# Order of one gate's last weight steps, and the slots of four small pieces, in the mLSTM heads of a hybrid layer

## The chip, the cores and the metric

One core of one Trainium2 chip runs one launch. The metric is the device time of that launch in microseconds. TensorE (PE in the profile) multiplies, VectorE (DVE) and ScalarE (ACT) prepare its operands and take its results, GpSimd (POOL) does a little, and the sync engine (SP) issues the loads of the weights.

## What is computed

One decoder layer on 256 tokens of width 4096: an RMSNorm, one wide input projection, two groups of heads (four mLSTM heads and a sparse attention), each with a SiLU gate, an output projection, the residual and a final RMSNorm. The change touches only the mLSTM heads. What one of these needs, cut from the reference:

```python
proj = rmsnorm(x, norm_gain) @ w_in
(m_q, m_k, m_v, m_o, m_z, m_i, m_f, ...) = split(proj)
qk = silu(causal_conv(concat(m_q, m_k), w_conv))        # four taps
# per head: 256 columns of q and of k, 512 of v, of the output gate m_o and of the other gate m_z
s   = (q @ k.T) * exp(dlog - m)                          # scores with the decay
num = s @ v ;  qn = sum(s)
h   = num / max(|qn|, exp(-m))
h   = sigmoid(m_o) * h
h   = h * rsqrt(mean(h * h) + eps) * mlstm_norm_gain
y_m = h * silu(m_z)
x   = x + concat(y_m, y_a) @ w_out
```

## The kernel before

Every large product is in float32 made of three passes: a matrix is kept as a high part and a low part (`hi` and `lo`), and TensorE adds high by high, high by low and low by high. The weights come as one long row of steps, each 128 by 1024 numbers (512 KB, two tiles of 512 columns), through a ring of four places (`RING`). SP loads a step into `w_raw` once DVE has done with the step four before it, ACT writes its high part into `w_hi` once TensorE has used the step four before it (`split`, L1253), and DVE writes the low part (`lo`, L1775). TensorE then uses it for both tiles of 128 tokens: an "eight", 4 products of 3 passes, 12 matmuls. In the loops ACT and DVE are three steps ahead of TensorE (`LOOKAHEAD`): at slot r they treat the weights of step r + 3, and then the small pieces that are written at slot r. TensorE issues the pieces that are written at step r ahead of step r's own matmuls. Each engine does its instructions strictly as written.

An mLSTM head is made in two blocks of 32 steps. `gates(h)` takes the weights of the output gate (block 0, banks `acc_a`) and of the other gate (block 1, `acc_b`); `keys(h)` takes those of the next head's queries and keys (block 0) and values (block 1). The loop runs `gates, keys` three times, and `gates(3)` stands behind it; the output projection (`B_OUT`) follows. In a `gates` block six of the sixteen pairs of weight tiles are not two eights but one "seven": seven products in place of eight, made of sums of weight tiles and sums of input tiles, which DVE and ACT have to make (`lo_seven`, `split_seven`). Its products go into the own banks and into four shared banks (`bank_xy`, which is bx and by, `bank_z`, `bank_v`). With `ORDER_M` the steps 0 to 5 of a gates block are eights (acc_a, acc_b in turn), step 6 and 7 are the first seven, 8 and 9 eights, 10 and 11 the next seven, and so on to step 27; 28 to 31 are eights.

Around the change the following happens in `gates(h)`. At step 0 TensorE makes the scores into bx. DVE multiplies them by the decay (slot 0, L2257), makes the low part of the values (slot 1, L2288) and of the scores (slot 2, `sw_lo`, L2262). At step `NUMERATOR` TensorE makes the numerators into by and bz and the sums into `bank_v`, 15 matmuls, and raises `num_ready`. DVE divides at slot `NUMERATOR + 1` (`normalise`, L2269 to L2275) and raises `hm_done`. Two others stand in wait for these: ACT may write the first seven's high sums (L1403) only after `num_ready`, since they lie on the scores and values, and TensorE may start the first seven's third product, the first that writes into by, only after `hm_done`:

```python
if first:
    wait_for(sums_free)          # gates: hm_done and s_lo_in
pe.wait_ge(t13_lo, n + 1)
passes(shared[P5][:, :], x_sum(S1), w_sum(0), first, final)
```

At the end of a block DVE adds the shared products up (`shared_products`, L2081, from slot 28) and then adds them to the own banks of block 0 (`own_sums(..., 0)`, L2087, slot 31) and of block 1 (slot 0 of the block behind). The next block's first eight writes into `acc_a` and waits for the first of these. In `keys(h)` the own sums of block 0 are made at slot 20, ACT scales them at slot 21 (`key_scale`, L1612), and TensorE transposes them at step `CONV_KEYS` = 22 (`conv_columns`, L763); the convolution's pieces on ACT and DVE follow at slots 22 to 29, the last being the low part of q and k (`qk_lo`, L2251), for which the next head's scores wait.

In `gates(3)` ACT and DVE also make the high and low part of the attention's output (`mix_hi`, L1313, and `mix_lo`, L1845), eight pairs of tiles, one at each of the slots 24 to 31 (`MIX_TAIL + c`). They overwrite the input tiles that this block is through with, and the output projection starts with them.

Of the kernel before, what the change touches and what calls it, by code (L numbers as in the profile page):

```python
# [86 lines left out]


MIX_EARLY, MIX_LATE = PAIRS - 2, 11
MIX_TAIL, MIX_TURN = 24, 1  # L90

MIX_M = PAIRS // 2

# [15 lines left out]
def interleaved(order):  # L109

    return tuple((c, h) for c in order for h in range(2))


def keys_first(quads):
# [59 lines left out]

GATES_KEYS, GATES_LAST = (0, 3, 4), (0, 2, 3)
PRODUCTS_KEYS, PRODUCTS_LAST = (2, 6, 10), (1, 4, 5)
SCORES, NUMERATOR = 0, 3
SUMS_GATES, SUMS_KEYS = 28, 18
CONV_V, CONV_KEYS = 1, 22
RESIDUAL = 12  # L180

WARM = 8
# [44 lines left out]
def hybrid_layer(nc, x, x_cols_first, w_all, final_norm_gain,  # L227
                 consts, early_consts, toe_bias, s_lo_kept, out):
    ctx = ExitStack()
    with ctx:  # L230
# [208 lines left out]
        def gates_two(h):  # L439

            return Two(4 * h * PAIRS + M0, 2 * h + 1, per_head * h + len(SEVEN), len(SEVEN),
                       interleaved(ORDER_M), (acc[0], acc[1]), [bx, by, bz, bv],
                       (kv_s_hi, m_s_lo), (m_t_hi, m_t_lo, m_t_raw))

        def keys_two(h):

            return Two(4 * h * PAIRS + (M0 + TWO_STEPS), 2 * h + 2, per_head * h + 2 * len(SEVEN),
                       FEW_V, keys_first(FEW_V), (acc[0], acc[1]), [bx, by, bz, bv],
                       (kv_s_hi, m_s_lo), (m_t_hi, m_t_lo, m_t_raw))
# [779 lines left out]
        def _(act):  # L1229
# [77 lines left out]
            def mix_hi(c):  # L1307

                w = gates_two(HEADS_M - 1)
                act.wait_ge(pe_used, w.start + w.steps.index((c, 1)) + 1)  # L1310
                if c < MIX_M:
                    act.wait_ge(az_free, GROUPS + 1)
                    act.activation(lhs_hi[:, 2 * c:2 * c + 2, :], mix_t[:, 2 * c:2 * c + 2, :],  # L1313
                                   ACT.Copy).then_inc(ht_hi, 1)
                    return
                act.wait_ge(ht_ready, c - MIX_M + 1)
                for k in range(2):
                    kk = 2 * c + k
                    last = act.activation(lhs_hi[:, kk, :], (by, bz)[c % 2][:, k * T:(k + 1) * T],
                                          ACT.Copy, scale=gain_mix[:, kk:kk + 1])  # L1320
                last.then_inc(ht_hi, 1)
# [227 lines left out]
            def head_pieces(h):  # L1549
# [88 lines left out]
                def gates_at(o, q, z):  # L1638
# [1 line left out]

                two_pieces = piece_map((0, values_hi), (SCORES, input_sums_lo), (SCORES + 1, sw_hi_part),
                                       (SUMS_GATES, gate_product))
                return two_pieces, conv_at, gates_at, (SUMS_KEYS, key_product), (CONV_KEYS - 1, key_scale)

            def gates(h, late={}, behind=None):
                found = head_pieces(h)[0]
                for c, more in late.items():
                    found.setdefault(c, []).extend(more)
                two_stream(gates_two(h), found, behind, (num_ready, h + 1))
# [15 lines left out]
                act.wait_ge(s_raw_done, SUM_ORDER.index(f) + 1)  # L1665
                act.activation(s_hi[:, f], s_raw[:, f], ACT.Copy).then_inc(s_hi_done, 1)

            gates(HEADS_M - 1, {MIX_TAIL + c: [lambda c=c: mix_hi(c)] for c in range(MIX_M)})
            last_gates = piece_map(*head_pieces(HEADS_M - 1)[2](*GATES_LAST))


# [80 lines left out]
        def _(dve):  # L1752
# [471 lines left out]
            def head_pieces(h):  # L2224
# [72 lines left out]
                def sums_at(w, c, last):  # L2297
                    return (*[(c + part // 2, lambda part=part: shared_products(w, m_shared, part))
                              for part in range(4)], (last, lambda: own_sums(w, 0)))
# [18 lines left out]
                def gates_at(o, z, y):  # L2318
# [3 lines left out]
                two_pieces = ((SCORES, scores), (SCORES + 1, values_lo), (SCORES + 2, scores_lo),  # L2322
                              (NUMERATOR + 1, lambda: normalise(0)),
                              (NUMERATOR + 1, lambda: normalise(1)),
                              *sums_at(gates_two(h), SUMS_GATES, SUMS_GATES + 3))
                return two_pieces, conv_at, gates_at, sums_at, own_sums

            def gates(h, late=(), behind=None):
                two_stream(gates_two(h), piece_map(*head_pieces(h)[0], *late), behind)

            def keys(h):
                _, _, gates_at, sums_at, own_sums = head_pieces(h)
                two_stream(keys_two(h), piece_map(
                    *gates_at(*PRODUCTS_KEYS), *sums_at(keys_two(h), SUMS_KEYS, CONV_KEYS - 2),
                    *head_pieces(h + 1)[1](CONV_KEYS)))
                own_sums(keys_two(h), 1)

# [20 lines left out]
                if f == SUM_ORDER[-1]:  # L2358
                    last.then_inc(s_lo_done, 1)

            gates(HEADS_M - 1, [(MIX_TAIL + c, lambda c=c: mix_lo(c)) for c in range(MIX_M)])
            late = piece_map(*head_pieces(HEADS_M - 1)[2](*PRODUCTS_LAST))
            for i, f in enumerate(SUM_ORDER):
                late.setdefault(SUMS + i, []).append(lambda f=f: input_sum(f))
# [231 lines left out]
def weight_stream(w_in, w_out, cmp_k_w1, cmp_v_w1):  # L2596


    def block(w, col, order=range(PAIRS)):
        pairs = w[:, col].reshape(PAIRS, 2, P, BW).transpose(0, 2, 1, 3).reshape(PAIRS, P, 2 * BW)  # L2600
        return [pairs[c] for c in order]

    def run(start):
        return np.arange(start, start + BW)

    def extra(i):
        found = np.zeros((P, 2 * BW), w_in.dtype)
        if i < SMALL_PAIRS:
            rows = w_in[i * SMALL_K * P:(i + 1) * SMALL_K * P]
            small = np.concatenate([rows[:, C_IF:C_IF + N_IF], rows[:, C_GATE:C_GATE + N_GATE]], axis=1)  # L2610
            found[:, 0:SMALL_K * N_SMALL] = small.reshape(SMALL_K, P, N_SMALL).transpose(
                1, 0, 2).reshape(P, -1)
            return found
        j, i = divmod(i - SMALL_PAIRS, CMP_PAIRS)
        w1 = (cmp_k_w1, cmp_v_w1)[j].reshape(2, CMP_PAIRS, CMP_PL, P, P)[:, i]
        return w1.transpose(2, 0, 1, 3).reshape(P, 2 * BW)

    kv = [block(w_in, run(C_KV + b * BW)) for b in range(6)]
    pairs = kv[0] + kv[1]
    pairs += [extra(i) if i is not None else kv[MIXED][c] for _, i, c in mixed_block()]  # L2620
    pairs += kv[3]
    for c in ORDER:
        pairs += [kv[4][c], kv[5][c]]
    pairs += block(w_in, run(C_AQ))
    for g in range(GROUPS):
        pairs += block(w_in, run(C_AZ + g * BW))
        if g < GROUPS - 1:
            pairs += block(w_in, run(C_AQ + (g + 1) * BW))
    def keys(h):
        q_k = np.concatenate([start + h * QK_M + np.arange(QK_M) for start in (C_MQ, C_MK)])  # L2630
        return [block(w_in, q_k), block(w_in, run(C_MV + h * BW))]

    pairs += sum(keys(0), [])
    for h in range(HEADS_M):
        gates = [block(w_in, run(col + h * BW)) for col in (C_MO, C_MZ)]
        pairs += [gates[i][c] for c, i in interleaved(ORDER_M)]
        if h < HEADS_M - 1:
            blocks = keys(h + 1)
            pairs += [blocks[i][c] for c, i in keys_first(FEW_V)]
    outs = [block(w_out, run(n * BW), [(c + PAIRS // 2) % PAIRS for c in range(PAIRS)])  # L2640
            for n in range(N_OUT)]
    pairs += outs[0]
    for p in range(TWOS):
        for c in ORDER:
            pairs += [outs[2 * p + 1][c], outs[2 * p + 2][c]]
    pairs += outs[N_OUT - 1]
    return np.concatenate(pairs)
# [33 lines left out]
```

## Time and profile before

| | us |
|---|---|
| median of 3 runs | 1752.58 |
| lowest and highest | 1752.17, 1753.28 |
| the profiled execution | 1752.96 |
| its span | 1751.2 |
| TensorE busy (matmuls) | 1733.5 (99%) |
| VectorE busy | 1313.6 (75%) |
| ScalarE busy | 947.6 (54%) |

The page's granted TensorE clock is full in every fortieth of the span. A matmul's record of 128x512 is 0.39 us long, while the next one starts 0.2267 us later: records overlap, so a wait shows in the distance of two starts, not in the busy share. The listed idle time in front of a matmul counts from the end of the record before; the time that was lost is longer by 0.39 - 0.2267 = 0.16 us. The gates and keys blocks of the four heads lie between 788 and 1399 us.

### The profile page before, as it was taken

To read this page: it belongs to the slowest core of one execution; us is meant where nothing else is said; L and a number is where in the kernel's file an instruction comes from. 1 tells how busy PE (TensorE), PEld (TensorE's weight loads), DVE (VectorE), ACT (ScalarE), POOL (GpSimd) and SP (SyncE) were. 2 spreads that over 40 slices of the span, in tenths; PEclk is the share of its full clock that TensorE was granted. 3 is DMA by queue.
4 is the path that set the end of the run, shared out by engine and by line. 5 is a ranking of instruction groups with operands and counts; after the bars stand their busy time and mean duration, and the time that the engine had idled before them with its cause. 6 is when DMAs were issued, how large, how long until landed. Compare 5 with 4: busy or idle time off the path is not lost.

```text
span 1751.2 us, 23455 instructions
## 1 busy us (share of the span) xinstructions
PE 1733.5 (99%) x8000; PEld 1437.0 (82%) x8000; DVE 1313.6 (75%) x1679; ACT 947.6 (54%) x1318; POOL 20.0 (1%) x33
## 2 busy tenths in 40 slices
PE   9999999999999999999999999999999999999997
PEld 7888888888888888888888888888888788888886
DVE  7556786566675756668887888788878988888876
ACT  7535555455555555545555555555555665564553
POOL 0000000000000000000000000000000000000000
PEclk9999999999999999999999999999999999999999
DMA  9657656545455454555646564666565656666674
GB/s 383 241 179 234 214 195 221 185 157 183 154 188 170 158 182 161 174 181 204 216 169 217 205 215 169 217 206 212 174 213 208 206 187 212 216 217 215 217 262 182
DMA packets 98325, 354.59 MB, mean 202 GB/s; under 512 B 10688, under 2 KB 11200, under 8 KB 97472
## 3 DMA queue, kind: packets, MB, share of 16 engines
q1 hardware_dynamic: 94480, 336.96, 55.7%
q10 hardware_dynamic: 3760, 16.52, 2.7%
q8 instruction: 51, 0.84, 0.2%
q14 instruction: 34, 0.28, 0.1%
HBM read 347.67 MB, written 5.77 MB: 202 GB/s over the span
## 4 chain that ended last, share of the span: by engine, by line
PE 88%; DVE 5%; DMA 3%; issue 2%; ACT 1%; SPq 0%; DVEq 0%; POOLq 0%; ACTq 0%; POOL 0%
PE acc_a L721 12%; PE acc_a L723 12%; PE acc_a L722 12%; PE acc_b L721 11%; PE acc_b L723 11%; PE acc_b L722 11%; DMA w_raw<-in_w_all 3%; PE bank_xy L721 3%; PE bank_xy L722 3%; PE bank_xy L723 3%; PE bank_z L723 1%; PE bank_z L721 1%; PE bank_z L722 1%; PE bank_v L722 1%; PE bank_v L723 1%
## 5 line engine op out<-in xcount | busy, mean ns | idle before, releaser
L1775 DVE TENSOR_TENSOR w_split<-w_raw,w_split 128x1024 fp32r<-128x1024 f32 x495 | 599.5, 1222 | 263.0 <-ACT w_split L1253 254.3
L1253 ACT ACTIVATE w_split<-w_raw 128x1024 fp32r<-128x1024 f32 x494 | 518.1, 1056 | 366.1 <-PE acc_b L723 176.8
L721 PE MATMUL acc_a<-w_split,lhs_hi 128*128 128x512 f32 x968 | 379.9, 392 | 2.6 <-DVE stage L2087 2.4
L723 PE MATMUL acc_a<-w_split,lhs_lo 128*128 128x512 f32 x968 | 377.2, 390 | 0.0
L722 PE MATMUL acc_a<-w_split,lhs_hi 128*128 128x512 f32 x968 | 377.2, 390 | 0.0
L721 PE MATMUL acc_b<-w_split,lhs_hi 128*128 128x512 f32 x890 | 348.4, 391 | 0.0
L723 PE MATMUL acc_b<-w_split,lhs_lo 128*128 128x512 f32 x890 | 346.6, 389 | 0.0
L722 PE MATMUL acc_b<-w_split,lhs_hi 128*128 128x512 f32 x890 | 346.5, 389 | 0.0
L721 PEld LDWEIGHTS acc_a<-w_split,lhs_hi 128*128 128x128 f32 x968 | 181.8, 188 | 39.6 <-issue 2.5
L723 PEld LDWEIGHTS acc_a<-w_split,lhs_lo 128*128 128x128 f32 x968 | 181.7, 188 | 38.5
L722 PEld LDWEIGHTS acc_a<-w_split,lhs_hi 128*128 128x128 f32 x968 | 181.9, 188 | 33.8
L723 PEld LDWEIGHTS acc_b<-w_split,lhs_lo 128*128 128x128 f32 x890 | 167.1, 188 | 35.1
L722 PEld LDWEIGHTS acc_b<-w_split,lhs_hi 128*128 128x128 f32 x890 | 167.2, 188 | 33.4
L721 PEld LDWEIGHTS acc_b<-w_split,lhs_hi 128*128 128x128 f32 x890 | 167.1, 188 | 33.2
L2038 DVE TENSOR_TENSOR w_split<-w_raw,w_split 128x1024 fp32r<-128x1024 f32 x120 | 114.2, 951 | 3.5 <-ACT w_split L1397 2.0
L1397 ACT ACTIVATE w_split<-w_raw 128x1024 fp32r<-128x1024 f32 x60 | 63.7, 1062 | 32.7 <-PE acc_a L723 16.7
L1403 ACT ACTIVATE m_t_hi<-m_t_raw 128x1024 fp32r<-128x1024 f32 x36 | 38.2, 1061 | 72.9 <-PE bank_z L723 40.5
L1410 ACT ACTIVATE m_t_hi<-m_t_raw 128x1024 fp32r<-128x1024 f32 x36 | 38.2, 1060 | 56.2 <-DVE m_t_raw L2062 56.2
L2067 DVE TENSOR_TENSOR m_t_lo<-m_t_raw,m_t_hi 128x1024 fp32r<-128x1024 f32 x36 | 44.1, 1226 | 17.9 <-ACT m_t_hi L1410 17.9
L2162 DVE TENSOR_TENSOR pt_lo<-bank_z,pt_hi 128x512 fp32r<-128x512 f32 (+1 forms) x32 | 17.9, 558 | 49.5 <-ACT pct L1487 49.5
L2047 DVE TENSOR_TENSOR m_t_raw<-w_raw 128x1024 f32<-128x1024 f32 x36 | 44.0, 1222 | 11.4 <-DMA w_raw<-in_w_all 7.4
L1485 ACT ACTIVATE pt_hi<-bank_z 128x512 fp32r<-128x512 f32 (+1 forms) x32 | 15.7, 491 | 66.8 <-PE bank_v L1067 66.8
(457 smaller groups left out, 2142.2 us busy)
## 6 DMA issues: line engine op xcount, KB each, us to landing
w_raw<-in_w_all SPq DMA_DIRECT2D x614, 512.0 KB
m_s_lo<-s_lo_kept ACTq DMA_DIRECT2D x4, 1536.0 KB, 7.5
wide<-in_x SPq DMA_DIRECT2D x8, 512.0 KB, 10.3
xres<-in_x ACTq DMA_DIRECT2D x8, 512.0 KB, 5.7
out_y<-wide SPq DMA_DIRECT2D x8, 512.0 KB, 3.6
gained_x<-in_x_cols_first SPq DMA_DIRECT2D x6, 512.0 KB, 7.5
toe<-in_toe_bias ACTq DMA_DIRECT2D x4, 512.0 KB, 5.0
gain_f<-in_final_norm_gain ACTq DMA_DIRECT2D x1, 2048.0 KB, 9.9
```

The lines of the kernel that those rows point to most:

```text
L721: pe.matmul(dst, a[0], b[0], start=start, stop=False)
L722: pe.matmul(dst, a[0], b[1], start=False, stop=False)
L723: return pe.matmul(dst, a[1], b[0], start=False, stop=stop)
L1253: act.activation(w_hi[:, cols], w_raw[:, cols], ACT.Copy).then_inc(hi_done, 1)
L1397: act.activation(w_hi[:, cols], w_raw[:, cols], ACT.Copy).then_inc(hi_done, 1)
L1403: act.activation(sum_hi[:, 0:2 * BW], sum_raw[:, 0:2 * BW], ACT.Copy).then_inc(t13_hi, 1)
L1410: act.activation(sum_hi[:, 2 * BW:].rearrange("p (i c) -> p i c", i=2), sum_raw[:, :].rearrange("p (i c) -> p i c", i=3)[:, 0:3:2, :], ACT ...
L1775: dve.tensor_tensor(w_lo[:, cols], w_raw[:, cols], w_hi[:, cols].bitcast(F32), ALU.subtract).then_inc(lo_done, 1)
L2038: return dve.tensor_tensor(w_lo[:, cols], w_raw[:, cols], w_hi[:, cols].bitcast(F32), ALU.subtract)
L2047: dve.tensor_tensor(sums[:, 0:2, :], tile(1, 0, 2).rearrange("p (i c) -> p i c", i=2), w_raw[:, 2 * s * BW:(2 * s + 4) * BW].rearrange("p ...
L2067: dve.tensor_tensor(sum_lo[:, 2 * BW:].rearrange("p (i c) -> p i c", i=2), sums[:, 0:3:2, :], sum_hi[:, 2 * BW:].bitcast(F32).rearrange("p ...
L2162: dve.tensor_tensor(in_batch(pt_lo, u), transposed_tiles(u), in_batch(pt_hi, u).bitcast(F32), ALU.subtract)
```

## The change

- The weights of a gates block come in another order at the end: of the last four eights (pairs 14 and 15) the two of the output gate now stand at steps 28 and 29, those of the other gate at 30 and 31 (`gates_in_turn`).
- DVE makes the own sums of the output gate at slot 30 in place of 31.
- `NUMERATOR` goes from 3 to 4: the numerators stand one eight later on TensorE, and the division on DVE stands at slot 5 in place of 4.
- `CONV_KEYS` goes from 22 to 23: the transposes of the next head's queries and keys and all convolution pieces stand one step later; the own sums at slot 20 and the scaling at slot 21 stay, now by the name `OWN_KEYS`.
- In `gates(3)` the conversions stand at slots 10, 14, 18, 22, 26, 28, 31 and 31 in place of 24 to 31.

```diff
-MIX_TAIL, MIX_TURN = 24, 1
+MIX_TAIL, MIX_TURN = (10, 14, 18, 22, 26, 28, 31, 31), 1
...
+def gates_in_turn(order):
+
+    last = order[-2:]
+    return interleaved(order[:-2]) + tuple((c, h) for h in range(2) for c in last)
...
-SCORES, NUMERATOR = 0, 3
+SCORES, NUMERATOR = 0, 4
 SUMS_GATES, SUMS_KEYS = 28, 18
-CONV_V, CONV_KEYS = 1, 22
+CONV_V, CONV_KEYS = 1, 23
+OWN_KEYS = 20
...
         def gates_two(h):
-                       interleaved(ORDER_M), (acc[0], acc[1]), [bx, by, bz, bv],
+                       gates_in_turn(ORDER_M), (acc[0], acc[1]), [bx, by, bz, bv],
...
-                return two_pieces, conv_at, gates_at, (SUMS_KEYS, key_product), (CONV_KEYS - 1, key_scale)
+                return two_pieces, conv_at, gates_at, (SUMS_KEYS, key_product), (OWN_KEYS + 1, key_scale)
...
-            gates(HEADS_M - 1, {MIX_TAIL + c: [lambda c=c: mix_hi(c)] for c in range(MIX_M)})
+            gates(HEADS_M - 1, piece_map(*[(MIX_TAIL[c], lambda c=c: mix_hi(c)) for c in range(MIX_M)]))
...
-                              *sums_at(gates_two(h), SUMS_GATES, SUMS_GATES + 3))
+                              *sums_at(gates_two(h), SUMS_GATES, SUMS_GATES + 2))
...
-                    *gates_at(*PRODUCTS_KEYS), *sums_at(keys_two(h), SUMS_KEYS, CONV_KEYS - 2),
+                    *gates_at(*PRODUCTS_KEYS), *sums_at(keys_two(h), SUMS_KEYS, OWN_KEYS),
...
-            gates(HEADS_M - 1, [(MIX_TAIL + c, lambda c=c: mix_lo(c)) for c in range(MIX_M)])
+            gates(HEADS_M - 1, [(MIX_TAIL[c], lambda c=c: mix_lo(c)) for c in range(MIX_M)])
...
-        pairs += [gates[i][c] for c, i in interleaved(ORDER_M)]
+        pairs += [gates[i][c] for c, i in gates_in_turn(ORDER_M)]
```

## Rows read from the trace of the kernel before

**Rows 1.** Busy time by stretch: length, PE, PEld, DVE, ACT, POOL, clock, DMA share, GB/s.
```profile
300.00:780.00 480.00, 480.00 (x2337) 402.78 (x2336) 309.26 (x554) 258.69 (x497) 9.67 (x4) 1.00 0.51 172
780.00:1410.00 630.00, 624.74 (x2792) 514.65 (x2791) 521.83 (x580) 344.52 (x399) 5.84 (x12) 1.00 0.58 202
```

**Rows 2.** What TensorE waited for, 780 to 1410 us: total us, times, longest.
```profile
PE acc_a L721 <- DVE stage L2087: 2.4, 4, 1.6
PE bank_xy L721 <- DVE sw_lo L2262: 1.6, 4, 0.6
PE bank_v L763 <- ACT stage L1612: 1.1, 2, 0.6
```

**Rows 3.** Timeline, TensorE, second head, numerators and first seven: start, us, instruction, idle before.
```profile
962.38 0.28 PE L721 MATMUL bank_xy<-qk_hi 128*128 128x256 f32 x1
...
972.67 0.49 PE L721 MATMUL bank_xy<-mv_hi,sw_hi 128*128 128x512 f32 x1 [0.58 <-DVE sw_lo L2262]
...
975.41 0.48 PE L721 MATMUL acc_b<-w_split,lhs_hi 128*128 128x512 f32 x1
...
985.03 0.39 PE L721 MATMUL bank_xy<-m_t_hi,in_s_hi 128*128 128x512 f32 x1
```

**Rows 4.** Timeline, ACT, same head: first seven's sums, then second seven's.
```profile
975.72 1.06 ACT L1403 ACTIVATE m_t_hi<-m_t_raw 128x1024 fp32r<-128x1024 f32 x1 [2.53 <-PE bank_v L1147]
...
991.77 1.06 ACT L1410 ACTIVATE m_t_hi<-m_t_raw 128x1024 fp32r<-128x1024 f32 x1 [1.50 <-DVE m_t_raw L2062]
992.74 1.04 ACT L1253 ACTIVATE w_split<-w_raw 128x1024 fp32r<-128x1024 f32 x1
```

**Rows 5.** Timeline, DVE, same head: first seven, division, second seven.
```profile
976.81 1.23 DVE L2057 TENSOR_TENSOR m_t_lo<-m_t_raw,m_t_hi 128x1024 fp32r<-128x1024 f32 x1 [0.26 <-ACT m_t_hi L1403]
978.07 0.69 DVE L2062 TENSOR_TENSOR m_t_raw<-w_raw,m_t_raw 128x512 f32<-128x512 f32 x1
...
981.19 0.15 DVE L2269 COPY den<-bank_v 128x2 f32<-128x2 f32 x1
...
982.73 0.74 DVE L2275 TENSOR_SCALAR hm<-bank_z,den 128x512 f32<-128x512 f32 x1
...
991.05 0.69 DVE L2062 TENSOR_TENSOR m_t_raw<-w_raw,m_t_raw 128x512 f32<-128x512 f32 x1
...
992.87 1.23 DVE L2067 TENSOR_TENSOR m_t_lo<-m_t_raw,m_t_hi 128x1024 fp32r<-128x1024 f32 x1 [0.53 <-ACT m_t_hi L1410]
994.01 2.38 DVE L1775 TENSOR_TENSOR w_split<-w_raw,w_split 128x1024 fp32r<-128x1024 f32 x2
```

**Rows 6.** Timeline, TensorE, first matmul behind the first and the last gates block.
```profile
876.06 0.50 PE L721 MATMUL acc_a<-w_split,lhs_hi 128*128 128x512 f32 x1 [0.29 <-DVE stage L2087]
...
1400.92 0.47 PE L721 MATMUL acc_a<-w_split,lhs_hi 128*128 128x512 f32 x1 [1.56 <-DVE stage L2087]
```

**Rows 7.** Timeline, DVE, end of the first gates block.
```profile
871.46 1.23 DVE L1775 TENSOR_TENSOR w_split<-w_raw,w_split 128x1024 fp32r<-128x1024 f32 x1
874.18 1.23 DVE L1775 TENSOR_TENSOR w_split<-w_raw,w_split 128x1024 fp32r<-128x1024 f32 x1 [1.50 <-ACT w_split L1253]
875.32 1.28 DVE L2087 TENSOR_TENSOR stage<-acc_a,stage 128x512 f32<-128x512 f32 x2
```

**Rows 8.** Timeline, DVE, last gates block: start of a seven, and a conversion.
```profile
1356.89 1.22 DVE L2047 TENSOR_TENSOR m_t_raw<-w_raw 128x1024 f32<-128x1024 f32 x1 [1.02 <-issue]
...
1398.36 0.68 DVE L1845 TENSOR_TENSOR lhs_lo<-wide,lhs_hi 128x512 fp32r<-128x512 f32 x1
```

**Rows 9.** Timeline, TensorE, transposes of keys, second time round the loop.
```profile
1108.05 0.39 PE L723 MATMUL acc_b<-w_split,lhs_lo 128*128 128x512 f32 x1
1108.56 0.65 PE L763 MATMUL bank_v<-c,stage 128*128 128x128 f32 x4
```

**Rows 10.** Timeline, DVE, last convolution piece, first time round.
```profile
956.73 1.22 DVE L2251 TENSOR_TENSOR qk_lo<-qk,qk_hi 128x1024 fp32r<-128x1024 f32 x1
```

**Rows 11.** Busy time by stretch, columns as in rows 1: the end, no matmul after 1741.0.
```profile
1745.00:1746.00 1.00, 0.00 (x0) 0.00 (x0) 1.00 (x3) 0.00 (x0) 0.00 (x0) 0.56 0.78 324
```

## The prediction

> **What bounds the kernel now.** I read the busy shares first. TensorE is busy 99% of the span, and in a long stretch without small pieces it is busy from end to end at the full granted clock; in the 630 us that hold the mLSTM heads 5.3 us are missing [rows 1]. So TensorE's own order of work is the bound, and this change, which gives it the same matmuls, can only move its waits. The waits view of that stretch names them all: four for the division's neighbour `sw_lo` (1.6 us in total), four for the own sums behind a gates block (2.4), two for the scaled keys (1.1) [rows 2]. A record outlasts the next start by 0.16 us, so each such wait costs 0.16 more than it is listed at; and the first record behind a wait is 0.50 or 0.49 long where 0.39 is usual [rows 3, 6], which I take as 0.1 us for getting going again. That makes 1.6 + 4 x 0.26 = 2.6 us, 2.4 + 1.0 = 3.4 us and 1.1 + 0.5 = 1.6 us.
>
> **The gate's order and the own sums at slot 30.** DVE now reads `acc_a` when step 29 is through, not step 30. In the first head DVE takes the weights of slot 30 from 871.46 to 872.69 and is then idle until 874.18 [rows 7]; the two sums (1.28 us [rows 7]) fit there and end at 873.9. TensorE wants them at 876.06 - 0.29 - 0.16 = 875.61 [rows 6], 1.7 us later. The three waits in the loop go: listed at 0.29 in the first, with 0.26 each on top, 3 x 0.55 = 1.65 us. DVE's next weights wait for ACT in any case (1.50 us idle at 874.18 [rows 7]), so nothing behind the moved piece gets late. The second gate's own sums stay where they were, and `acc_b` is first written at step 4 of the keys block.
>
> **The conversions of the last block.** The fourth wait is the long one, 1.56 listed at 1400.92 [rows 6], because DVE has eight conversions of 0.68 us [rows 8] among the last eight slots. Spread, five of them stand one to each seven. There DVE is idle for 1.02 us ahead of the next seven's first sum, waiting for its weights [rows 8], and a conversion fits in. Two are left at slot 31, behind the own sums. I put this part at the whole wait, 1.56 + 0.26 = 1.8 us. If the cover were gone, the five would put DVE 5 x 0.68 = 3.4 us behind and the wait could stay: between 0 and 1.8 us, and I take the upper end since the idle time stands in the rows. ACT's half is hidden with more room: it is busy 55% here [rows 1]. The input tiles that are overwritten belong to steps already passed at these slots, so ACT does not wait for TensorE.
>
> **The transposes at step 23.** The scaled keys come at the same slot, and TensorE asks one eight (12 x 0.2267 = 2.72 us) later; the longest of the two waits was 0.6 [rows 2]. They go. But also where nothing is waited for, the transposes start 1108.56 - 1108.05 - 0.23 = 0.28 us late [rows 9], and this stays. With 0.16 a wait on top, the gain is 1.1 + 2 x (0.16 - 0.28) = 0.9 us. The convolution's chain on ACT and DVE goes one slot later. Its end, `qk_lo`, started at 956.73 and ended at 957.95, and the scores that wait for it stood at 962.38 [rows 10, 3]: 4.4 us, less one step of 2.72 and 0.4 for TensorE's gain leaves 1.3 us. Hidden, but with less room; cover gone, it would cost at most what is over.
>
> **The numerators at step 4.** In the second head step 2 ends at 972.67 - 0.58 - 0.16 = 971.93, the numerators start 0.74 late and step 3 starts at 975.41 [rows 3]. After, step 3 fills this time, `sw_lo` has been there for 2 us, and the four waits of 2.6 us in total go. But what is behind the numerators has come nearer. Call their end T. Before, three eights and six matmuls of the seven lay between T and the first write into by: 985.03 - 975.41 = 9.62 us [rows 3]. After it is two eights: 9.62 - 2.72 = 6.90 us. In that time the division must be made, and its engine has this queue, as soon as `num_ready` is up:
>
> ACT's L1403 starts at T + 0.31 [rows 3, 4]; DVE's L2057 1.09 us later [rows 4, 5]; L2062 1.26 later [rows 5]; ACT's L1410 0.72 after that starts (991.05 to 991.77), and DVE's L2067 1.10 after L1410 [rows 4, 5]. That is T + 4.48. L2067 and a weight conversion L1775 each hold DVE for 1.14 us from start to start (992.87 to 994.01 [rows 5]). At slot 4 the division came at once. At slot 5 it stands behind the weights of step 8, for which ACT starts 0.97 after L1410 (991.77 to 992.74 [rows 4]), at T + 4.35, in time. So the division starts at T + 4.48 + 1.14 + 1.14 = T + 6.76. It lasts from 981.19 to 983.47, 2.28 us [rows 5], and ends at T + 9.04; TensorE goes on 0.10 later (875.32 + 0.64 to 876.06 [rows 6, 7]). It arrives at T + 6.90 and waits **2.24 us**, plus 0.1 for the restart, in each of the four heads: 9.4 us. Before, the same wait had 9.62 - (983.47 - 975.41) = 1.56 us of room; a step less for TensorE and a weight step more ahead of DVE use it up and more. Behind the wait nothing else is late: the seven's other sums and steps 8 and 9 are prepared meanwhile. The bounds: 1.8 if the chain runs closer than these rows, 2.6 if each of the four hand-overs costs 0.1 more.
>
> **The sum.** Gone: 2.6 + 1.65 + 1.8 + 0.9 = 6.95 us. New: 9.4 us. Net +2.4 us. The profiled execution took 1752.96 us with a span of 1751.2, 0.38 above the median of the three runs; it would become 1755.4. Against the median of 1752.58 my forecast is **1755.0 us**, +0.14%. Its own range: the new wait 4 x 0.4 either way, the last block's gain from 0 to 1.8, gives 1753.4 to 1758.4.
>
> **The rivals.**
> *The last block's conversions cost what they should give.* Each now stands ahead of a seven's first sum, and if the weights come sooner than in the row there is no idle time of 0.68 us or more to hold it. DVE then gets later with each seven, and the own sums at slot 30 still end after TensorE's last eight. It decides from the point where the idle time of 1.02 us [rows 8] falls below 0.68. The gain of 1.8 goes: 1756.8 us, slower than before by 0.24%. Against it speak the row itself and that the wait for weights comes from DVE's own release of the ring.
> *The division is in time after all.* That needs a chain shorter by 2.24 us. Only the conversion of step 8's weights (1.14) could be out of its way, and the program has it ahead. If DVE and ACT ran without the gaps between records, the wait might be 1.1 us: 4 x 1.1 less, 1750.6 us. With no wait at all, which would be the change doing just what its parts say, 1752.6 - 6.95 = 1745.6 us. Against it: each distance above was seen between just these instructions.
> *The clock falls in the new waits.* After the last matmul, at 1741.0, the granted clock fell only between 1745 and 1746 (0.56, between the two levels of 2.4 and 1.2 GHz) [rows 11]; with ten shorter waits in the heads it stayed 1.00 [rows 1]. A wait of 2.24 us is longer than any of these. If the 21 matmuls of the seven behind it ran at the lower level they would take 4.8 us more, four times: 1774 us. The Trainium skill (TensorE: Matmul & The Clock Gate, "A second HAM failure mode: psum-queue depth-cycling") states that short idle times between groups of matmuls can be enough to let the clock swing between its levels; by that rule this rival would be the likely one. The trace so far disagrees, at 1.00 with all ten waits.
> *The numerators' or scores' operands come late.* `qk_lo` has 1.3 us of room left, and `sw_lo` more; below nought the convolution's shift would cost its excess in three heads, some 1 us each at most.
>
> **How the numbers follow.** Chances: my forecast 0.68; the last block's rival or another loss of its size 0.13; a shorter wait (around 1750.6) 0.09; no wait (1745.6) 0.05; the clock 0.02; late operands 0.03. The range for 8 in 10 takes the forecast's own with a little to the lower side, for the shorter wait, and leaves out the ends: 1752.6 to 1758.4. About 0.2% (3.5 us: below 1749.1, above 1756.1) is what a measurement of this kernel can tell from no change. Faster: the case without a wait and part of the short one, 0.08. Slower: the last block's rival, the clock and the upper part of my own range, 0.22. The same: 0.70.
>
> **What would show it.** In the waits of TensorE, `sw_lo` L2262, `stage` L2087 and `stage` L1612 are gone or nearly, and a new line stands there: bank_xy L721 waiting for `hm` (L2275), four times, some 2.1 us listed each. TensorE's busy time in the heads falls short of the stretch by some 8.6 us rather than 5.3. The time line of DVE at the first seven shows L2067, L1775, L2269 in this order and L2269 6.8 us behind the numerators' end. The last block has a conversion in each gap ahead of L2047, and the block's end without a wait. Were that line for `hm` missing, the step on the division is wrong and the time is near 1746; were the L2087 wait still 1.5 us at the last block, the cover was not there; a granted clock below 1.00 in the heads would be the clock's case.

## The result, and the profile after

The changed kernel takes 1760.4 us at the median (1759.2 to 1762.9 in six runs) against 1752.2 (1751.8 to 1753.3): 1.0048 times, 95% interval 1.0038 to 1.0059. It is slower by 8.2 us, clear of the noise, where 2.4 were forecast. Its profiled execution took 1759.5 us with a span of 1757.7. Two later executions were far slower, one of the kernel before (2493.9 us, mean clock 0.654) and one of the spread conversions alone (2170.7 us, 0.752), and they are in no ratio below.

What TensorE waited for between 780 and 1420 us, in the changed kernel (total us, times, longest; in this kernel's line numbers, which are 7 higher), against [rows 2]:

```profile
PE bank_xy L728 <- DVE hm L2282: 8.5, 4, 2.2
PE acc_a L728 <- DVE w_split L1782: 0.9, 3, 0.3
```

The three kinds of wait of before are gone. A new one for the division stands in their place, and a smaller one, for weights, that was not there. The time line of TensorE in the second head, against [rows 3]:

```profile
976.06 0.39 PE L728 MATMUL bank_xy<-mv_hi,sw_hi 128*128 128x512 f32 x1
...
978.69 0.48 PE L728 MATMUL acc_a<-w_split,lhs_hi 128*128 128x512 f32 x1
...
985.37 0.39 PE L730 MATMUL acc_a<-w_split,lhs_lo 128*128 128x512 f32 x1
987.97 0.47 PE L728 MATMUL bank_xy<-m_t_hi,in_s_hi 128*128 128x512 f32 x1 [2.22 <-DVE hm L2282]
...
989.42 0.62 PE L728 MATMUL acc_b<-w_split,in_s_hi 128*128 128x512 f32 x1
989.84 0.63 PE L729 MATMUL acc_b<-w_split,in_s_hi 128*128 128x512 f32 x1
990.26 0.63 PE L730 MATMUL acc_b<-w_split,m_s_lo 128*128 128x512 f32 x1
```

The numerators start without a wait and end at T = 978.69. The write into by, 42 matmuls behind T before, is 30 behind it now and waits 2.37 us (from the start before it, 985.37, to 987.97, less the 0.2267 that a matmul takes). The waits of the first and the third head are as long, that of the last head is 2.01 us. Then something else: from 989.42 on the matmuls start 0.43 us apart in place of 0.2267. VectorE's queue behind T, against [rows 5]:

```profile
981.35 0.69 DVE L2069 TENSOR_TENSOR m_t_raw<-w_raw,m_t_raw 128x512 f32<-128x512 f32 x1
...
983.17 1.23 DVE L2074 TENSOR_TENSOR m_t_lo<-m_t_raw,m_t_hi 128x1024 fp32r<-128x1024 f32 x1 [0.53 <-ACT m_t_hi L1417]
984.31 1.22 DVE L1782 TENSOR_TENSOR w_split<-w_raw,w_split 128x1024 fp32r<-128x1024 f32 x1
985.45 0.15 DVE L2276 COPY den<-bank_v 128x2 f32<-128x2 f32 x1
...
986.98 0.74 DVE L2282 TENSOR_SCALAR hm<-bank_z,den 128x512 f32<-128x512 f32 x1
```

L2074, the weights of step 8, then the division, which starts at T + 6.76 and ends at T + 9.03. TensorE's granted clock in stretches behind the four waits (the clock is the third number from the end), first to fourth head:

```profile
812.40:815.80 3.40, 3.40 (x15) 2.83 (x16) 3.37 (x4) 0.00 (x0) 0.00 (x0) 1.00 0.47 172
989.40:992.80 3.40, 3.40 (x9) 2.64 (x8) 2.42 (x3) 0.00 (x0) 0.00 (x0) 0.50 0.45 154
1165.30:1168.70 3.40, 3.40 (x15) 2.83 (x16) 3.37 (x4) 0.00 (x0) 0.00 (x0) 1.00 0.48 160
1341.20:1344.50 3.30, 3.30 (x9) 2.60 (x8) 3.27 (x4) 0.00 (x0) 0.00 (x0) 0.51 0.47 159
```

In the second and the fourth head eight matmuls ran at 1.2 GHz, half the full level: 9 starts in a stretch where the first head has 15. Each of these two falls cost 1.7 us. The one in the last head stands behind the shortest of the four waits.

### Where the time went

I took the starts of the same matmuls in both traces and looked where their distance changes (us, later than before):

```
                                     head 1  head 2  head 3  head 4     sum
numerators and wait for hm            +1.92   +1.53   +1.52   +1.56    +6.5
the clock behind it                    0      +1.71    0      +1.75    +3.5
first matmul of the next block        -0.63   -0.58   -0.62   -1.84    -3.7
inside the keys block, steps 4 to 19  +0.66   +0.59   +0.65            +1.9
transposes of the keys                -0.73   -0.33   -0.84            -1.9
```

With 0.2 from before the first head these are the 6.5 us between the spans 1751.2 and 1757.7. The six runs of the changed kernel show the falls as well: mean clocks of 0.996 (1759.2 to 1759.7 us, three runs), 0.995 (1761.1) and 0.994 (1762.7, 1762.9), steps of 1.6 us, so two, three and four falls. Two is what the trace shows; three and four are counted from the times. Without them it would take 1756.0 us.

### The profile page after: what moved, and what is told of

It is laid out like the page before. It is cut to its first block, busy times and chain, and to the rows that moved or that the text cites. A ratio compares the mean times of both kernels' runs of the same rounds, so it can differ in the third digit from the quotient of the medians.

```text
span 1757.7 us, 23455 instructions
## 1 busy us (share of the span) xinstructions
PE 1736.4 (99%) x8000; PEld 1440.6 (82%) x8000; DVE 1313.3 (75%) x1679; ACT 946.0 (54%) x1318; POOL 20.1 (1%) x33
## 4 chain that ended last, share of the span: by engine, by line
PE 68%; issue 29%; DMA 1%; DVE 1%; ACT 0%; POOL 0%; SPq 0%; POOLq 0%; DVEq 0%; ACTq 0%
PE acc_a L728 9%; PE acc_a L730 9%; PE acc_a L729 9%; PE acc_b L728 8%; PE acc_b L730 8%; PE acc_b L729 8%; PE bank_xy L728 2%; PE bank_xy L730 2%; PE bank_xy L729 2%; DMA w_raw<-in_w_all 1%; PE bank_z L730 1%; PE bank_z L729 1%; PE bank_z L728 1%; PE bank_v L729 1%; PE bank_v L730 1%
## 5 line engine op out<-in xcount | busy, mean ns | idle before, releaser
L2064 DVE TENSOR_TENSOR m_t_lo<-m_t_raw,m_t_hi 128x1024 fp32r<-128x1024 f32 x36 | 44.0, 1222 | 20.0 <-ACT m_t_hi L1410 19.9
L2074 DVE TENSOR_TENSOR m_t_lo<-m_t_raw,m_t_hi 128x1024 fp32r<-128x1024 f32 x36 | 44.1, 1226 | 18.9 <-ACT m_t_hi L1417 18.9
```

The source lines that it names most:

```text
L2064: dve.tensor_tensor(sum_lo[:, 0:2 * BW], sum_raw[:, 0:2 * BW], sum_hi[:, 0:2 * BW].bitcast(F32), ALU.subtract).then_inc(t13_lo, 1)
L2074: dve.tensor_tensor(sum_lo[:, 2 * BW:].rearrange("p (i c) -> p i c", i=2), sums[:, 0:3:2, :], sum_hi[:, 2 * BW:].bitcast(F32).rearrange("p ...
```

## The experiments

The first four were run together, the kernel before at 1752.1 us; the next four at 1752.2; the last four at 1751.9.

### The changed kernel with the numerators back

```diff
-SCORES, NUMERATOR = 0, 4
+SCORES, NUMERATOR = 0, 3
```

> The changed kernel with the numerators back at step 3 and the division at slot 4, all else kept. Theory A (the step on the numerators costs it all: a wait for the division of 2.4 us less the wait of before, 6.5 us in four heads, and a fall of the clock behind some of these waits, 1.7 us each): the changed kernel's 1760.4 us less 6.5 and less all falls of the clock, that is before plus 0.2 - 1.8 (gates waits) + 1.9 (given back in the keys blocks) - 1.8 (last block) - 1.9 (transposes) = 1748.8 us, no wait for hm, mean clock 0.998 as before, four waits for sw_lo again. Rival B (the other parts cost something too, the new order of the weights above all): 1752 us or more, with waits elsewhere.

Measured: 1750.0 us, 0.9988 of the kernel before (0.9979 to 0.9997), clock 0.998 to 0.999. TensorE's waits in its trace:

```profile
PE bank_xy L728 <- DVE sw_lo L2269: 1.9, 4, 0.9
PE bank_v L777 <- DVE warm L1830: 1.4, 1, 1.4
PE acc_a L728 <- DVE w_split L1782: 1.1, 4, 0.3
```

One figure in the change costs 10.3 us, and the rest of it gains 2.1. Rival B is out: no wait was added but the one for weights (the one of 1.4 us for `warm` stands in the first microseconds and is in the kernel before too). The gain is 1.3 us short of theory A, for a reason that the later runs show.

### The numerators' step alone

```diff
-SCORES, NUMERATOR = 0, 3
+SCORES, NUMERATOR = 0, 4
```
(on the kernel before)

> The kernel before with the numerators at step 4 and the division at slot 5, nothing else. Theory A: before plus 6.5 us for the four waits, plus 1.7 us for each of them behind which the clock falls (two to four): 1762 to 1765.5 us, mean clock 0.994 to 0.996, four waits for hm of 2.2 us listed. Rival B (it takes the other parts to make it slow): 1752 to 1757 us.

Measured: 1762.7 us (1762.0 to 1763.8), 1.0062 (1.0048 to 1.0076), clock 0.995 to 0.996. It needs none of the other parts. Its trace has the waits for `hm` of 2.37, 2.37, 2.37 and 2.01 us and two falls of the clock, in the third and fourth head this time, so again behind one of the three waits of 2.37 us and behind the one of 2.01 (columns as above):

```profile
1165.20:1169.70 4.50, 4.50 (x13) 3.54 (x14) 3.83 (x4) 0.00 (x0) 0.00 (x0) 0.62 0.46 147
1342.50:1347.20 4.70, 4.70 (x14) 3.69 (x15) 4.03 (x4) 0.00 (x0) 0.00 (x0) 0.64 0.47 165
```

Theory A holds. And its last block, with the eight conversions where they were, shows another thing:

```profile
PE bank_xy L721 <- DVE hm L2275: 8.5, 4, 2.2
...
PE acc_a L721 <- DVE stage L2087: 1.3, 4, 0.4
```

The wait for the own sums at the last block, 1.56 listed in the trace of before [rows 6], is here 0.39. So the long wait that I had read belongs to that execution, and not to each.

### The division one slot earlier

```diff
-                              (NUMERATOR + 1, lambda: normalise(0)),
-                              (NUMERATOR + 1, lambda: normalise(1)),
+                              (NUMERATOR, lambda: normalise(0)),
+                              (NUMERATOR, lambda: normalise(1)),
```

> The changed kernel with the division at slot 4 in place of 5, ahead of step 8's weights on DVE, the numerators still at step 4. The wait for hm should become 2.37 - 1.14 = 1.2 us. Theory A1 (the clock falls only behind a wait longer than some length that lies above 1.2 us): 1760.4 - 4 x 1.14 - 2 to 4 x 1.7 = 1749 to 1752.5 us, clock 0.998. Rival A2 (any new wait at this place can bring the clock down, whatever its length): 1756 us with a clock of 0.995, the waits alone gone by 4.6 us.

Measured: 1751.8 us (1751.6 to 1753.6), ratio to before 1.0000 (0.9991 to 1.0009), clock 0.998 to 0.999 in eleven runs.

```profile
PE bank_xy L728 <- DVE hm L2282: 3.9, 4, 1.1
```

The waits fell from 2.37 to 1.24 us (from 2.01 to 0.87 in the last head), and the trace has no fall of the clock. With one weight conversion less ahead of the division 8.6 us are gone, 4.6 by waiting and some 4 by the clock: A1.

### The order of the gate's weights alone

```diff
-                       interleaved(ORDER_M), (acc[0], acc[1]), [bx, by, bz, bv],
+                       gates_in_turn(ORDER_M), (acc[0], acc[1]), [bx, by, bz, bv],
...
-                              *sums_at(gates_two(h), SUMS_GATES, SUMS_GATES + 3))
+                              *sums_at(gates_two(h), SUMS_GATES, SUMS_GATES + 2))
```
(and the same order in `weight_stream`, on the kernel before)

> The kernel before with the output gate's last two eights first and its own sums at slot 30, nothing else. Theory C (the keys block is bound by DVE, so what TensorE gains ahead of it comes back as a wait for weights around step 18): the three waits in the loop go (-1.8 us) and come back as waits for w_split (+1.9 us); the last block's wait goes too, because the own sums now stand ahead of two conversions (-1.8 us): 1750.5 us. Rival D (my prediction's view, the keys block has room): 1748.6 us. Rival E (the last wait needs the spread conversions): 1752.3 us.

Measured: 1751.5 us (1751.0 to 1752.2), 0.9996 (0.9987 to 1.0005).

```profile
PE acc_a L727 <- DVE w_split L1781: 0.9, 3, 0.3
PE bank_v L769 <- ACT stage L1618: 0.9, 1, 0.9
```

No wait for the own sums is left, at the last block neither, and three waits for weights at step 18 of the keys blocks are there. Between this kernel and the one before TensorE is some 0.6 us earlier at each keys block's start and back where it was, or 0.04 later, at its step 19. The time alone lies between those of theory C and rival E, and its interval includes no change; it is the trace that decides. Theory C is right for the loop: the order gains nothing there. Rival E is out: the order with the own sums at slot 30 ends the last block's wait without the spread conversions. That this gain lasts because no seven follows at once behind that block was not tested.

### A division a little longer

```diff
                     if t == 1:
+                        link(last)
+                        last = dve.tensor_scalar(hm[:, t, 0:P], (by, bz)[t][:, 0:P],
+                                                 den[:, t:t + 1], None, ALU.mult)
                         last.then_inc(hm_done, 1)
```
(with the division at slot 4; the number of links per head is one more)

> The changed kernel with the division at slot 4, as in the run before, and 128 columns of its last product written a second time, to lengthen the wait for hm in each head: 1.25 us (0.87 in the last head) plus some 0.4 to 0.5, so about 1.7 us. Theory F (a wait of this length does not yet bring the clock down; the kernel before had one of 1.72 us at the last block and kept its clock): 1751.8 + 4 x 0.45 = 1753.6 us with a clock of 0.998, no matmul at twice the distance. Rival G (the fall depends on the place, behind the numerators' short matmuls, more than on the length): two to four falls of 1.7 us, 1757 to 1760.5 us, clock 0.996 to 0.994.

Measured: 1753.5 us (1753.0 to 1755.1), 1.0008 (0.9999 to 1.0017), clock 0.998 or 0.999 in eleven runs. Waits of 1.62, 1.63, 1.61 and 1.26 us, no fall in the trace. F, not G: same place, same short matmuls ahead, no fall. A wait of more than 2 us at another place was not tried.

### A division longer by a whole product

The same edit with all 512 columns, the division at slot 5.

> The changed kernel with the last product of the division written twice: the wait for hm goes from 2.37 to about 3.2 us in each head. Theory F (the longer the wait, the more surely the clock falls behind it): a fall in every head and every run, 1756.2 (the changed kernel without falls) + 4 x 0.85 + 4 x 1.7 = 1766.4 us, clock 0.994 in each run, little spread. Rival G (length has no say): falls in two to four heads as in the changed kernel, 1763 to 1766.4 us with the same spread.

Measured: 1765.8 us (1765.2 to 1767.1), clock 0.994 in four runs and 0.993 in one. Waits of 3.16 us (2.79 in the last head), and a fall in each of the four heads (the third line is the second head again, over the whole of its slow stretch):

```profile
813.50:817.50 4.00, 4.00 (x12) 3.20 (x13) 3.83 (x4) 0.00 (x0) 0.00 (x0) 0.65 0.41 135
991.20:995.20 4.00, 3.99 (x10) 3.13 (x11) 3.85 (x4) 0.00 (x0) 0.00 (x0) 0.50 0.41 131
990.40:997.30 6.90, 6.09 (x15) 4.80 (x16) 4.65 (x5) 0.00 (x0) 0.00 (x0) 0.51 0.29 99
1170.50:1174.50 4.00, 4.00 (x11) 3.19 (x12) 3.85 (x4) 0.00 (x0) 0.00 (x0) 0.60 0.39 131
1348.20:1352.20 4.00, 4.00 (x11) 3.13 (x12) 3.97 (x4) 0.00 (x0) 0.00 (x0) 0.58 0.38 138
```

In the second head fourteen matmuls ran at the low level and cost 2.9 us, where the other three falls cost 1.5 to 1.8. The clock was low there before the wait was over, from 990.4 on with the wait's end at 991.21. This profiled run is the slowest of the five and the one with 0.993. Theory F holds in how often the clock falls, but the price of a fall isn't fixed at 1.7 us.

### Between the two

The same whole product twice, with the division at slot 4.

> The changed kernel with the division at slot 4 and the whole last product written twice: a wait for hm between the 1.62 us that never brought the clock down (run with the short repeat) and the 2.37 us that did in two to four heads of four. Expected wait 2.05 us (1.7 in the last head), 1753.5 + 4 x 0.43 = 1755.2 us without falls, plus 1.7 us for each. If how often the clock falls grows with the length: none to two falls, 1755.2 to 1758.6 us. If the fall has a fixed length above 2.05 us: none in any run, clock 0.998.

Measured: 1757.7 us (1756.6 to 1758.9), 1.0033 (1.0020 to 1.0046), clocks of 0.998, 0.997 and 0.996. Waits of 2.03 us (1.66 in the last head). Against 1755.2 us without falls these times are one or two falls. The trace has one, in the second head:

```profile
812.70:816.70 4.00, 4.00 (x18) 3.31 (x19) 3.97 (x5) 0.31 (x1) 0.00 (x0) 1.00 0.46 145
987.90:992.80 4.90, 4.88 (x15) 3.87 (x16) 4.87 (x5) 0.00 (x0) 0.00 (x0) 0.65 0.55 143
```

The kernels that move the division, together, by the waits of the first three heads and of the last, and by the falls:

```
wait, heads 1 to 3 / head 4     in the traces                           by the runs' times and clocks
1.24 / 0.87, 1.62 / 1.26        0 of 8                                  none in 22 runs
2.03 / 1.66                     1 of 4 (a 2.03)                         1 or 2 in each of 6 runs
2.37 / 2.01 (two kernels)       4 of 8 (two of six 2.37, both 2.01)     2 to 4 in each of 11 runs
3.16 / 2.79                     4 of 4                                  4 in each of 5 runs
```

Longer waits bring more falls, but between 2.01 and 2.37 us the length doesn't decide alone: both waits of 2.01 us in a trace had a fall behind them, and four of six of 2.37 had none. What else decides is left open. The right-hand column is the weaker one. A mean clock of three digits doesn't tell one fall from none (the trace with one fall has 0.998, as the runs without), and one run of the kernel before shows 0.947 at an ordinary 1753.4 us. The times do tell them apart, by 1.7 us a fall, except for single runs: the slowest of the 22 in each of its two groups is 1.6 to 1.8 us above its median, as some runs of the kernel before are.

### The output product off the keys block's queue

```diff
-PRODUCTS_KEYS, PRODUCTS_LAST = (2, 6, 10), (1, 4, 5)
+PRODUCTS_KEYS, PRODUCTS_LAST = (2, 6, 16), (1, 4, 5)
...
-                    *gates_at(*PRODUCTS_KEYS), *sums_at
+                    *gates_at(*PRODUCTS_KEYS), (17, lambda: dve.wait_ge(ym_done, h + 1)), *sums_at
```
(on the changed kernel with the numerators back; the added line makes VectorE wait for this product to be finished before it goes on to the sums at slot 18)

> The kernel with the numerators back at step 3, and the head's output product (L2316 of the changed kernel, 1.3 us on VectorE) moved in the keys block from slot 10 to slot 16, behind the last seven and step 18's weights. Theory C (VectorE's queue bounds the first 18 steps of the keys block, and this product is part of it): the three waits for w_split at step 18 (0.43 to 0.46 us over, and their restart) go, 1750.0 - 1.3 = 1748.7 us at least, and the time gained is still there at the end of the keys block. Rival H (the weights' loads bound it, VectorE only follows them): the waits stay, 1750.0 us.

Measured: 1748.2 us (1747.7 to 1750.0), 0.9979 (0.9970 to 0.9988). VectorE between step 16 and step 20 of the first keys block, first in the changed kernel, then in this one:

```profile
910.73 1.23 DVE L2074 TENSOR_TENSOR m_t_lo<-m_t_raw,m_t_hi 128x1024 fp32r<-128x1024 f32 x1 [0.53 <-ACT m_t_hi L1417]
911.88 1.41 DVE L2316 SCALAR_TENSOR_TENSOR wide<-hm,hr,m_gate 128x512 f32 x2
913.20 2.35 DVE L1782 TENSOR_TENSOR w_split<-w_raw,w_split 128x1024 fp32r<-128x1024 f32 x2
915.47 1.22 DVE L2054 TENSOR_TENSOR m_t_raw<-w_raw 128x1024 f32<-128x1024 f32 x1
```

```profile
908.91 1.23 DVE L2074 TENSOR_TENSOR m_t_lo<-m_t_raw,m_t_hi 128x1024 fp32r<-128x1024 f32 x1 [0.52 <-ACT m_t_hi L1417]
910.05 2.35 DVE L1782 TENSOR_TENSOR w_split<-w_raw,w_split 128x1024 fp32r<-128x1024 f32 x2
913.31 1.23 DVE L2054 TENSOR_TENSOR m_t_raw<-w_raw 128x1024 f32<-128x1024 f32 x1 [0.91 <-issue]
```

In the changed kernel nothing is idle there: TensorE starts its first eight behind the seven at 914.48, just when the first of the two weight conversions is through. With the output product moved VectorE has 0.91 us to spare and the three waits are gone. C, not H.

### The scores' low part one slot earlier

```diff
-                              (SCORES + 2, scores_lo)
+                              (SCORES + 1, scores_lo)
```
(on the kernel of the run before)

> As the run before, and with the low part of the scores made at slot 1 of the gates block, behind the values' low part and ahead of step 5's weights. The waits for sw_lo (1.9 us listed, 2.5 with what lies over, 2.9 with the restarts) should go, since sw_lo is then made 1.1 us earlier and the longest of them is 0.86: 1748.7 - 2.7 = 1746.0 us. Rival: the values' low part or step 3's weights come last then, and 0.1 to 0.5 us of each wait stays: 1747 to 1748 us.

Measured: 1744.9 us (1744.7 to 1745.4), 0.9958 (0.9945 to 0.9972): 7.3 us faster than the kernel before. Of these, 3.4 us came with this edit, from 1748.2. It takes away the same wait that the numerators' later step was to fill, without bringing the division's reader nearer. All waits of its span:

```profile
PE bank_v L777 <- DVE warm L1830: 1.4, 1, 1.4
PE acc_a L728 <- DVE w_split L1782: 0.4, 2, 0.2
PE acc_a L790 <- ACT w_split L1331: 0.2, 1, 0.2
```

### The spread conversions alone, and the fastest kernel without them

```diff
-MIX_TAIL, MIX_TURN = 24, 1
+MIX_TAIL, MIX_TURN = (10, 14, 18, 22, 26, 28, 31, 31), 1
```
(alone, on the kernel before; then undone in the kernel of the run above)

> The kernel before with the last block's conversions at slots 10 to 31 in place of 24 to 31, nothing else; the own sums stay at slot 31. If VectorE's lateness at the last block comes from the conversions alone, the wait there falls from 1.72 us to the 0.45 us that the other three blocks show: 1752.2 - 1.3 = 1750.9 us. If spreading them makes VectorE late elsewhere: 1752.2 us or more, with new waits between 1340 and 1400 us.

> The fastest kernel so far (numerators at step 3, output product at slot 16, scores' low part at slot 1) with the conversions put back to slots 24 to 31. With the own sums at slot 30 ahead of the conversions written there, as in the run of the order alone, no wait is expected at the last block's end: 1744.9 us, the spread conversions worth nothing by then. Rival: the conversions delay VectorE so that a wait of 0.5 to 1.7 us is back: 1745.4 to 1746.6 us.

Measured: 1752.3 us alone, ratio 1.0000 (0.9990 to 1.0010), and 1745.0 us without them in the fastest kernel, 0.9961 against 0.9958. The spreading is worth nothing in either. The conversions did find room, as forecast: the last four sevens' first sums sat idle for 0.8 us together in the trace of the spreading alone, against 1.6 to 4.1 us in the three traces with the conversions at slots 24 to 31 and the own sums at slot 31 (idle times like the one of 1.02 us in [rows 8]). But the time gains nothing by it. In the trace of the spreading alone the last block's wait is 0.38 as listed, but traces without it show 0.39 too (the numerators' step alone, above, and the transposes alone, below).

### The later transposes alone

```diff
-CONV_V, CONV_KEYS = 1, 22
+CONV_V, CONV_KEYS = 1, 23
+OWN_KEYS = 20
```
(and `OWN_KEYS` for the own sums and the scaling, on the kernel before)

> The kernel before with the transposes and the convolution one step later, nothing else. My prediction took 0.28 us of each late start as not to be had and put the part at 0.9 us: 1751.3 us. By the starts of the changed kernel (938.42 behind 938.19) there is no such rest, and the part is 0.65 + 0.28 + 0.76 = 1.7 us with 0.2 for the restarts: 1750.3 us.

Measured: 1750.6 us (1749.9 to 1751.4), 0.9992 (0.9982 to 1.0001): a gain of 1.4 us at the median, with an interval that just includes no change. In the changed kernel the transposes start at the ordinary distance behind the last matmul:

```profile
938.19 0.39 PE L730 MATMUL acc_b<-w_split,lhs_lo 128*128 128x512 f32 x1
938.42 0.60 PE L770 MATMUL bank_v<-c,stage 128*128 128x128 f32 x4
```

The late start of 0.28 us that I had read in the second keys block of the kernel before [rows 9] was a wait for the scaling, whose end stands at 1108.12:

```profile
1106.80 1.32 ACT L1612 ACTIVATE stage<-stage,rstd 128x512 f32<-128x512 f32 x2
```

TensorE starts 0.44 us behind this end, and 0.43 behind it in the other two keys blocks (933.79 to 934.22 and 1283.06 to 1283.49), where the view lists a wait.

## Why the prediction failed, step by step

**The numerators' step** was right in its mechanism and nearly in size: the division at T + 6.76 as worked out, its end at T + 9.03 for T + 9.04, the wait 2.37 us for 2.24, since the hand-over to TensorE took 0.25 and not 0.10. In the sum +6.5 us for +6.8 (9.4 less 2.6).

**The clock** is what failed. It stood among the rivals with a chance of 2 in 100 and a price of 4.8 us a head. I set the chance by ten waits that kept the full clock, and the longest was 1.72 us; the new wait, 2.37, lay outside of what these rows can say, and I had said so. What it did cost is 1.7 us a fall, eight matmuls and not twenty-one, in two to four heads of a run: 3.4 to 6.8 us, and 4.4 at the median, the larger part of the 5.4 by which the forecast was short. So the step that failed is the one that left the clock's term out of the sum, on the strength of shorter waits. The section of the Trainium skill that I had cited against the change (TensorE: Matmul & The Clock Gate, "A second HAM failure mode: psum-queue depth-cycling") tells of small idle times between groups of matmuls, frequent enough that the clock swings between its levels. It held in direction only: idle times between groups did bring the clock down here, but each fall in the heads stands behind a single wait of 2 us or more, and ten waits of 0.3 to 1.7 us did nothing.

**The order of the gate's weights** was forecast at 1.65 us in the loop. The three waits went (1.83 by the starts) and 1.9 came back inside the keys block. The step that failed is "nothing behind the moved piece gets late": I had looked at VectorE's next instruction and not at its whole queue up to step 19. The rows were to be had: before the change, too, VectorE went from 899.1 to 925.9 us with two idle times of 0.53 us, both for a rounding of ScalarE's, and TensorE's first eight behind the seven started 0.07 us late at 912.35 (0.30 behind the matmul before it, less 0.2267), right behind the first of the two weight conversions that began at 911.08:

```profile
908.61 1.22 DVE L2067 TENSOR_TENSOR m_t_lo<-m_t_raw,m_t_hi 128x1024 fp32r<-128x1024 f32 x1 [0.53 <-ACT m_t_hi L1410]
909.75 1.41 DVE L2309 SCALAR_TENSOR_TENSOR wide<-hm,hr,m_gate 128x512 f32 x2
911.08 2.35 DVE L1775 TENSOR_TENSOR w_split<-w_raw,w_split 128x1024 fp32r<-128x1024 f32 x2
...
919.42 1.23 DVE L2067 TENSOR_TENSOR m_t_lo<-m_t_raw,m_t_hi 128x1024 fp32r<-128x1024 f32 x1 [0.53 <-ACT m_t_hi L1410]
```

A reader that is on time by nothing has no room to take a gain.

**The last block's conversions** were put at 1.8 us. The wait that the term was made of was 1.72 us long in the profiled execution and 0.54 or 0.55 in three traces of other kernels that keep its own sums at slot 31, with and without the spreading. The typical value of the term is about 0.6, and the own sums at slot 30 give it alone. This also accounts for nearly all of the 1.3 us by which the kernel with the numerators back fell short of theory A. The three runs of before lay between 1752.2 and 1753.3 and the profiled one near the upper end; that could have warned me.

**The transposes** were put at 0.9 us, and 1.9 came between the traces of before and after, 1.4 in the run alone. I had taken 0.28 us of each late start as a price of transposing. It was a wait, too short to be listed.

Summed up: without falls the changed kernel takes 1756.0 us, 3.8 over before, where I had 2.4; the 1.4 are the keys block (+1.9) and the last block (+1.2) less the transposes (-1.0) and smaller terms (-0.7 together). Up to there the range would have held it. The numerators' step and the transposes were forecast by the right mechanism; the order, the last block and above all the clock were not. The rival on the last block's conversions was wrong (they found their room), and so was the one on a division in time; `qk_lo` was not late anywhere.

## What to carry to other kernels

Moving a producer one step later on the engine that is the bound shortens the way to the next reader of its results by that step, and a piece bound to it by a slot number moves behind more work on its own engine: count both ways before the move, and rather make the operand earlier than its user later (here `sw_lo` one slot earlier gained 3.4 us; the numerators one step later lost 10.3). A gain on the bound engine is only worth what the next stretch can take; look for the place where another engine's queue has no idle time and its reader is on time by nothing. And where a new wait would be longer than any wait in the trace, the trace says nothing about the clock behind it: give that case a real chance, and its price in matmuls at half rate.

## What was not expected of the hardware

- A single TensorE wait of 2.01 to 2.37 us between long dense stretches could halve its granted clock (1.00 to 0.50) for eight matmuls, 1.7 us, and did so behind some of the waits of a run and not behind others of the same length: 2, 3 or 4 of 4, by which the runs of one kernel differ by up to 3.7 us. None of the traces shows it behind a wait of 1.72 us or less, and the one with waits of 2.79 and 3.16 us shows it behind all four.
- The low level set in only 1.45 us after the wait's end in the second head (987.97 to 989.42), so the slow matmuls stand away from the wait. In the second head of the kernel with waits of 3.16 us it had set in 0.8 us before the wait's end, and fourteen matmuls ran at it and not eight.
- The wait at the end of the last block differed by 1.2 us between executions with the same code around it. Why VectorE was late in one and not in others is left open. In the trace of before it sat idle ahead of the first sums of the last four sevens for 4.1 us in all, at least once for the weights' load; in two traces of other kernels with the conversions at slots 24 to 31 and the own sums at slot 31 it was 2.7 and 1.6 us. Weights that arrive later in some executions would fit, but no run tests it.
